# A two-layer transformer stack: inputs sent in pieces between the first weight units, modulation tiles and weight conversions placed between the rows of the first norm

## The reference, cut to what matters

```
m = silu(cond) @ ada_w[layer] + ada_b[layer]        # 3072 values, once for x and once for ctx
shift, scale, gate = split(m, 3)
h = rms_norm(x, norm_g) * (1 + scale) + shift       # 1024 wide; the same for ctx with its own values
x = x + gate * mixer(h)
```

## Time and profile before

| what | us |
|---|---|
| runs | 2254.93, 2245.04, 2248.68 (median 2248.68) |
| the profiled execution: its own time | 2256.99 |
| its span, first to last instruction | 2254.8 |
| busy: TensorE | 1992.5 (88%) |
| busy: VectorE | 1171.8 (52%) |
| busy: ScalarE | 887.4 (39%) |
| busy: GpSimd | 694.8 (31%) |
| mean granted TensorE clock | 0.926 |

### The profile page before, as it was taken

The page is one execution under the profiler, slowest core; times in us unless marked ns, Lnnn a source line. Parts: engine busy times, 40 slices in busy tenths (PEclk is TensorE's granted clock), DMA queues, the critical chain, the costliest instruction groups (busy, mean ns, idle before and its releaser), DMA issues.

```text
span 2254.8 us, 27585 instructions
## 1 busy us (share of the span) xinstructions
PE 1992.5 (88%) x10708; PEld 1606.3 (71%) x10708; DVE 1171.8 (52%) x1657; ACT 887.4 (39%) x1199; POOL 694.8 (31%) x310
## 2 busy tenths in 40 slices
PE   4899999999787977976683999999999999999996
PEld 3687677777666867764472788788778877878875
DVE  2422666664276757657799334225444464522442
ACT  3252656654334453443331444234432234422432
POOL 1121011102214223222235344344344443444432
PEclk6799999999978989878796999999999999999998
DMA  7111211212211100112120222223223322323331
GB/s 277 38 56 54 76 48 67 76 67 85 59 37 37 39 29 29 38 52 80 37 76 10 84 84 94 88 96 98 84 87 101 93 89 90 94 84 94 94 94 47
DMA packets 46257, 166.80 MB, mean 74 GB/s; under 512 B 5392, under 2 KB 5520, under 8 KB 45872
## 3 DMA queue, kind: packets, MB, share of 16 engines
q1 hardware_dynamic: 44208, 158.88, 22.1%
q10 hardware_dynamic: 1920, 6.16, 0.8%
HBM read 162.92 MB, written 2.10 MB: 73 GB/s over the span
## 4 chain that ended last, share of the span: by engine, by line
PE 75%; DVE 17%; ACT 4%; issue 2%; DMA 1%; POOL 0%; ACTq 0%; DVEq 0%
PE ps L454 20%; PE ps L455 20%; PE ps L456 20%; PE ps L559 4%; PE ps L572 2%; PE ps L589 2%; DVE ex L1210 2%; DVE sq L1210 2%; DVE hf L1210 2%; ACT sq L831 1%; DVE tmp L1210 1%; PE ps L488 1%; DVE acc L1210 1%; PE ps L476 1%; DVE wS L1605 1%
## 5 line engine op out<-in xcount | busy, mean ns | idle before, releaser
L1194 POOL TENSOR_TENSOR wlo<-raw,whi 128x1024 fp32r<-128x1024 f32 x251 | 607.7, 2434 | 1303.8 <-ACT whi L814 1303.8
L814 ACT ACTIVATE whi<-raw 128x1024 fp32r<-128x1024 f32 x251 | 257.7, 1055 | 669.1 <-PE ps L456 647.2
L454 PE MATMUL ps<-Ahi,whi 128*128 128x512 f32 (+1 forms) x784 | 320.1, 408 | 27.5 <-issue 11.9
L455 PE MATMUL ps<-Alo,whi 128*128 128x512 f32 (+1 forms) x784 | 314.9, 402 | 0.0
L456 PE MATMUL ps<-Ahi,wlo 128*128 128x512 f32 (+1 forms) x784 | 313.5, 400 | 0.0
L1210 DVE TENSOR_TENSOR ps<-ps,rstd 128x1024 f32<-128x1024 f32 (+1 forms) x60 | 69.7, 1162 | 263.8 <-PE ps L456 227.3
L454 PEld LDWEIGHTS ps<-Ahi,whi 128*128 128x128 f32 x784 | 154.8, 197 | 72.5 <-issue 23.0
L454 PE MATMUL ps<-Fhi,whi 128*128 128x512 f32 x416 | 167.5, 403 | 13.1 <-DVE Flo L1210 12.9
L456 PEld LDWEIGHTS ps<-Ahi,wlo 128*128 128x128 f32 x784 | 154.6, 197 | 33.7
L455 PEld LDWEIGHTS ps<-Alo,whi 128*128 128x128 f32 x784 | 154.9, 198 | 32.1 <-issue 0.5
L1216 DVE SCALAR_TENSOR_TENSOR cv<-ps,vec,cv 128x511 f32<-128x511 f32 (+1 forms) x176 | 131.9, 749 | 71.6 <-ACT cv L831 66.9
(11 more groups left out here) (252 smaller groups left out, 3919.9 us busy)
## 6 DMA issues: line engine op xcount, KB each, us to landing
raw<-in_units SPq DMA_DIRECT2D x299, 512.0 KB, 3.7
X<-in_xT ACTq DMA_DIRECT2D x1, 2048.0 KB, 12.8
out_xT<-X SPq DMA_DIRECT2D x8, 256.0 KB, 2.1
CX<-in_ctxT ACTq DMA_DIRECT2D x1, 1024.0 KB, 15.7
masks<-in_masks ACTq DMA_DIRECT2D x1, 512.0 KB, 3.5
acc<-in_rope ACTq DMA_DIRECT2D x1, 384.0 KB, 3.0
gmw<-in_gmw ACTq DMA_DIRECT2D x1, 384.0 KB, 2.9
bs<-in_bs ACTq DMA_DIRECT2D x1, 384.0 KB, 3.5
```

The lines of the kernel that those rows point to most:

```text
L454: nc.tensor.matmul(out, sh, mh, start=first, stop=False)
L455: nc.tensor.matmul(out, sh, ml, start=False, stop=False)
L814: nc.scalar.activation(whi[:, s % CONV, :], raw[:, c % RAW, :], ACT.Copy).then_inc(sem("whi"), 1)
L1194: nc.gpsimd.tensor_tensor(wlo[:, s % CONV, :], raw[:, plan.unit_at[("split", s)] % RAW, :], whi[:, s % CONV, :].bitcast(fp32), ALU.subtrac ...
```

## The change

1. **Input and constants.** X and CX are no longer sent by ScalarE's queue. SP sends them in four pieces of two rows each (256 KB a row of X, 128 KB a row of CX), piece i ahead of unit i+1. ScalarE's queue sends vec, sel, eps1, ident; `vec` has a semaphore of its own, and the first LOG_EXP table load goes.
2. **Order of the modulation tiles.** `ADA` orders them by row: shift 0, scale 0, shift 1, scale 1 and so on, then the gates of layer 0 and all of layer 1. `sc1` is made per scale tile, in `ada_t`. The norm's sum n0 comes after tile 1 and not after tile 7.
3. **VectorE's prologue.** One square sum, tiles 0 and 1, the other sums; then for each further tile its copy, the bias of the tile before, and one row.
4. **A row** is two instructions for hf = (X·sc1)·rstd, ScalarE adds the shift while it rounds (`shifted`, two instructions in place of one), and the remainder is (hf + shift) - high in two instructions in place of one.
5. **First weights.** Units 0, 1 and 2 of the converted weights are converted by ScalarE after rows 4, 5 and 6 (at most one each), and lowered by GpSimd then; before, all three came ahead of the norm's root.
6. **Attention and second norm.** Twelve modulation tiles stay in attention (both of pairs 0, 4, 5 and 6, that of q = 4 in pairs 1, 2 and 3, that of q = 0 in pair 7). The last four, tiles 8 to 11 of layer 1 (its gates), move behind l0: three ahead of the sum n1, one behind it, then their `ada_t`. Their units now stand between l0's and r's in the load order.

```
+ADA = [(0, 0), (0, 4), (0, 1), (0, 5), (0, 2), (0, 6), (0, 3), (0, 7)]
+ADA += [(0, j) for j in range(8, 12)] + [(1, j) for j in range(12)]
+ADA_BESIDE = {(p, q): i + 8 for i, (p, q) in enumerate([(0, 0), (0, 4), (1, 4), (2, 4), (3, 4), (4, 0), (4, 4), (5, 0),
+                                                        (5, 4), (6, 0), (6, 4), (7, 0)])}
+SS_AFTER = 1
+INPUTS_AT = {1: 0, 2: 1, 3: 2, 4: 3}
...
         for m in range(8):
             tile(("l0", m), [("residc", m + 1)], ktiles("wout0", m))
+        for i in range(20, 23):
+            ada(i)
         norm("n1")
+        ada(23)
+        for i in range(20, 24):
+            ada_t(i)
...
             for c, (kind, i) in enumerate(plan.units):
+                if c in INPUTS_AT:
+                    two = slice(2 * INPUTS_AT[c], 2 * INPUTS_AT[c] + 2)
+                    sy.dma_start(X[:, two, :], a["xT"][:, two, :]).then_inc(sem(f"in{INPUTS_AT[c]}"), 16)
+                    sy.dma_start(CX[:, two, :], a["ctxT"][:, two, :]).then_inc(sem(f"in{INPUTS_AT[c]}"), 16)
...
-            for j in range(8):
-                ada(0, j)
-                if j == 0:
-                    pe.wait_ge(sem("consts"), 16 * 4)
+            for i in range(8):
+                ada(i)
+                if i == 0:
+                    pe.wait_ge(sem("consts"), 16 * 3)
+                    pe.wait_ge(sem("ones"), 2)
                 else:
-                    ada_t(0, j - 1)
-            ada_t(0, 7)
-            pe.wait_ge(sem("ones"), 2)
-            norm("n0")
+                    ada_t(i - 1)
+                if i == SS_AFTER:
+                    norm("n0")
+            ada_t(7)
...
-                    if q in (0, 4):
-                        ada(*more[2 * p + q // 4])
-                    if q in (2, 5):
-                        ada_t(*more[2 * p + q // 4])
+                    if (p, q) in ADA_BESIDE:
+                        ada(ADA_BESIDE[p, q])
+                    if (p, q // 4 * 4) in ADA_BESIDE and q in (2, 5):
+                        ada_t(ADA_BESIDE[p, q // 4 * 4])
...
-            ac.dma_start(X[:, :, :], a["xT"]).then_inc(sem("xl"), 16)
-            ac.dma_start(CX[:, :, :], a["ctxT"]).then_inc(sem("cl"), 16)
-            nc.scalar.preload_act_table_set(LOG_EXP)
...
+            def shifted(layer, dst):
+
+                ac.wait_ge(sem("hf"), split[0] + 1)
+                k, b = dst
+                for c, cols in enumerate([slice(0, T), slice(T, N)]):
+                    act(b[:, k, cols], hf[:, split[0] % 2, cols], ACT.Identity, mod[:, layer, 2 * k + c:2 * k + c + 1], 1.0,
+                        "hi" if c else None)
+                split[0] += 1
+
+            squares("n0", both, lambda k: [(f"in{k // 2}", 32)])
+            ac.wait_ge(sem("consts"), 48)
+            root("n0", False)
             for k in range(KD):
-                high(Hhi[:, k, :])
+                shifted(0, (k, Hhi))
+                if k in (4, 5, 6):
+                    convert(plan.index[("adaT", 7)], 1)
...
+                if shift is None:
+                    tt(lo, hf[:, i % 2, 0:lo.shape[-1]], hi.bitcast(fp32), SUB, "lo")
+                else:
+                    for c, cols in enumerate([slice(0, T), slice(T, N)]):
+                        stt(lo[:, cols], hf[:, i % 2, cols], shift[:, c:c + 1], hi[:, cols].bitcast(fp32), ADD, SUB,
+                            "lo" if c else None)
...
+            def modulated(layer, k, hi, lo):
+                b = to_split(N)
+                for c, (src, cols) in enumerate([(X, slice(0, T)), (CX, slice(T, N))]):
+                    stt(b[:, cols], src[:, k, :], sc1[:, layer, 2 * k + c:2 * k + c + 1], rstd[:, cols], MUL, MUL,
+                        "hf" if c else None)
+                queued(hi[:, k, :], lo[:, k, :], mod[:, layer, 2 * k:2 * k + 2])
...
+            def ada_t(i):
+                layer, j = ADA[i]
+                ps = psum(("adaT", i))
                 tt(mod[:, layer, 4 * j:4 * j + 4], ps[:, 0:4], v_(f"ada_b{layer}", 4 * j, 4), ADD, "mod")
+                if 4 <= j < 8:
+                    c = slice(4 * j - 16, 4 * j - 12)
+                    stt(sc1[:, layer, c], mod[:, layer, 4 * j:4 * j + 4], 1.0, v_(f"norm_g{layer}", 4 * j - 16, 4), ADD, MUL)
...
-            ve.wait_ge(sem("consts"), 64)
-            sums("n0")
-            for j in range(8):
-                ada(0, j)
-                if j:
-                    ada_t(0, j - 1)
-            ada_t(0, 7)
-            scales(0)
-            modulated("n0", 0, Hhi, Hlo)
+            ve.wait_ge(sem("vec"), 16)
+            ada(0)
+            sums("n0", [1])
+            ada(1)
+            ada_t(0)
+            sums("n0", range(2, 8))
+            for i in range(2, 9):
+                if i < 8:
+                    ada(i)
+                ada_t(i - 1)
+                if i == 2:
+                    ve.wait_ge(sem("n_rs"), 2)
+                modulated(0, i - 2, Hhi, Hlo)
+            modulated(0, 7, Hhi, Hlo)
+            flush()
...
             sums("n1")
-            modulated("n1", 1, Ahi, Alo)
+            for i in range(20, 24):
+                ada(i)
+            ve.wait_ge(sem("n_rs"), 2 * NI["n1"] + 2)
+            for k in range(KD):
+                modulated(1, k, Ahi, Alo)
+                if k >= 4:
+                    ada_t(16 + k)
+            flush()
```

More of the change, by code:

```diff
@@ L127, in ada, with ada_t @@
                 self.ada += 1
-            tile(("ada", layer, j), [("arow", 12 * layer + j + 1)], slots=slots)
-        def ada_t(layer, j, slots=None):
-            tile(("adaT", layer, j), [("mod", 12 * layer + j + 1)], slots=slots)
+            tile(("ada", i), [("arow", i + 1)], slots=slots)
+        def ada_t(i, slots=None):
+            tile(("adaT", i), [("mod", i + 1)], slots=slots)
         def ktiles(name, m, k=KD):
@@ L173, in out @@
             tile(("O", p, q), [("og", TN * p + q + 1)], slots=[2])
-        more = [(0, j) for j in range(8, 12)] + [(1, j) for j in range(12)]
         score(0)
@@ L490, in ada @@
                 done(last)
-            def ada_t(layer, j):
-                ps = tile(("adaT", layer, j))
-                pe.wait_ge(sem("arow"), 12 * layer + j + 1)
+            def ada_t(i):
+                ps = tile(("adaT", i))
+                pe.wait_ge(sem("arow"), i + 1)
                 for m in range(2):
-                    last = nc.tensor.matmul(ps[:, 2 * m:2 * m + 2], arow[:, (2 * (j % 2) + m) * P:(2 * (j % 2) + m + 1) * P], sel[:, :],
+                    last = nc.tensor.matmul(ps[:, 2 * m:2 * m + 2], arow(i)[:, m * P:(m + 1) * P], sel[:, :],
                                             start=True, stop=True)
@@ L502, in _ @@
             pe.wait_ge(sem("cnd"), 1)
-            for j in range(8):
-                ada(0, j)
-                if j == 0:
-                    pe.wait_ge(sem("consts"), 16 * 4)
-                else:
-                    ada_t(0, j - 1)
-            ada_t(0, 7)
-            pe.wait_ge(sem("ones"), 2)
-            norm("n0")
+            for i in range(8):
+                ada(i)
+                if i == 0:
+                    pe.wait_ge(sem("consts"), 16 * 3)
+                    pe.wait_ge(sem("ones"), 2)
+                else:
+                    ada_t(i - 1)
+                if i == SS_AFTER:
+                    norm("n0")
+            ada_t(7)
             for m in range(5):
@@ L1223, in _, with sums @@
             nsq = [0]
-            def sums(name):
+            def sums(name, ks=None):
                 i = NI[name]
@@ L1231, in sums @@
                     ve.wait_ge(sem("psum"), plan.index[("ss", NORMS[i - 1][0])] + 1)
-                for k in range(1, k_):
+                for k in ks or range(1, k_):
                     ve.wait_ge(sem("n_sq"), nsq[0] + per * (k + 1))
@@ L1380, in _ @@
                         k_odd(p + 1)
-                    if q in (0, 4):
-                        ada(*more[2 * p + q // 4])
-                    if q in (2, 5):
-                        ada_t(*more[2 * p + q // 4])
+                    if (p, q) in ADA_BESIDE:
+                        ada(ADA_BESIDE[p, q])
+                    if (p, q // 4 * 4) in ADA_BESIDE and q in (2, 5):
+                        ada_t(ADA_BESIDE[p, q // 4 * 4])
             out(PAIRS - 1, TN - 1)
-            scales(1)
             def resid(key, m, gate=None, n_sem="resid"):
@@ L1400, in _ @@
             sums("n1")
-            modulated("n1", 1, Ahi, Alo)
+            for i in range(20, 24):
+                ada(i)
+            ve.wait_ge(sem("n_rs"), 2 * NI["n1"] + 2)
[4 more added lines that the diff above has]
+            flush()
+            ts(small2[:, 0:1], eps1[:, 0:1], 1.0, None, MUL, s="n_use")
             def decay(h, d):
```

96 lines of the change are left out of this document (42 added, 54 removed).

## The result

Measured with the kernel before on one chip, in turn: 2226.47 us (median of 4 runs, 2220.24 to 2230.62) against 2246.96, ratio 0.9894 with a 95% interval of 0.9866 to 0.9921, 20.5 us faster. The three have a mean of 25.7; 28.5 was predicted (2220.2 from the median shown). The profiled execution took 2220.24 us, with a span of 2218.5.

A forecast was written before the change was run, and what follows sets the result against it. TensorE was taken to bound mid-attention (busy 97.6 of 100 us), chains of waits the start and second norm. Gains of 18.5 + 6.5 + 3.5 = 28.5 us gave 2228.5 for the profiled execution, 2220.2 from the median; range 2210 to 2236.

The forecast's parts named there:

- Arrival and the norm: Start: tile 1's second unit lands near 15.2 us, square sums end near 24 (29.2 before), row 0 follows at 30.
- Rows between tiles: Prologue: VectorE sets the pace from 35.7 us, 2.6 us per row, rounds of 3.3; last remainder at 56.7 without collisions.
- Collisions: Rows 5 to 7: GpSimd's three lowerings and VectorE shut each other out, 7.0 us taken (bounds 0 and 7.0; 4.6 as seen).
- the first rival: Rows 5 to 7: lowerings beside VectorE cost nothing, 7.0 us more gained, gain 35.5, 2213 us; chance 0.16.
- c0: First product tile after the rows: ends between 64.7 and 66.4 us, 65.4 taken, against 83.9 before.
- First term: Start through the end of c0: 18.5 us gained, bounds 13 and 26.
- Attention: Four tiles taken out: three pairs give 2.1 us each, 6.3 together, and pair 7 gives 0.2.
- second term: Attention with four modulation tiles taken out: 6.5 us gained, bounds 0 and 10.
- The second rival: Attention gives nothing back, since ScalarE and VectorE pace its pairs and tiles filled holes: gain 22, 2226.7 us; chance 0.12.
- Second norm: Behind l0: shorter rows give 4.1 us, the fourth tile takes 0.5; 3.5 us gained, bounds 1 and 5.
- The rival on the other side: Slower: ScalarE's conversions in attention and at the second norm wait 4.7 us each for loads, 37.6 in all, 2257.8; chance 0.04.
- the third rival: Start: input pieces arrive out of order, sums 3.8 us late, late units 6.4 more; gain 18.3, 2230.4 us; chance 0.08.

The follow-up runs named there:

- The three: Changed kernel, unaltered, against the kernel before in three sets of runs on different chips: 20.5, 34.2 and 22.4 us faster.
- the second: Changed kernel, unaltered, against the kernel before once more on another chip: 2220.66 us (5 runs) against 2254.83 (11 runs), ratio 0.9853.

## Why the prediction was right

- **Arrival and the norm.** Tile 1's last unit landed at 17.0, not 15.2. The estimate took the bytes ahead of it over 0.40 MB/us; the third slice of 2.75 us has a dip to 201 that the kernel before doesn't have the earlier trace rows, some 0.5 MB or 1.4 us. It stands at 191 to 219 in all eleven profiles with the pieces in this order, at 285 with the pieces one unit earlier, and in neither of the two of the kernel before; why is open. GB/s in 40 slices of the changed kernel's first 110 us:

```profile
GB/s 53 375 201 398 419 419 416 413 307 0 6 179 374 334 389 393 356 273 0 191 21 173 34 162 0 0 191 0 0 191 0 6 186 4 0 182 9 0 0 6
```

The sums took 5.93 us as forecast and ended at 25.3, 1.3 late; row 0 began 1.6 late.
- **Rows between tiles.** 56.7 was forecast for the last remainder without collisions. Measured are 64.1 less 6.0, 58.1: 1.4 late, which the late arrival accounts for (row 0 was 1.6 late). Each three-operand instruction took 0.752 and 0.485 us, as the earlier trace rows had it, and three rounds of 3.3 us were seen as 3.27, 3.47 and 3.27. A unit's landing held a tile by only 0.17 us (at 43.50).
- **Collisions.** 7.0 was taken, 4.6 and 0 were the other values. It was 6.0, 2.0 per lowering (5.9 by the kernel without conversions between the rows, counted from row 5's start): the VectorE instruction that a lowering meets runs on to its end, up to 0.2 us, and the next one is held and ends 0.3 to 0.6 us after the lowering. VectorE had no idle time in which any of it could hide. By the rule of the Trainium skill ("SBUF — State Buffer", section "SBUF: two separate sides"), a VectorE instruction with two inputs in on-chip memory and a GpSimd one that reads it shut each other out, and the one that starts first holds the shared ports for its whole duration. The trace agrees, with 2.44 and 2.60 us in place of 0.485 beside lowerings of 2.42 and 2.38. That the collisions cost nothing, the first rival, is thereby out.
- **c0.** Forecast 65.4, measured 66.3, 65.1 and 66.8. That it comes so near is in part luck: the late arrival (1.4 to 1.6) and the smaller collisions (1.0) nearly cancel. First term 18.2 against 18.5. Of it the old rows would lack 3.8, by one run; the remaining 14.4 are the order.
- **Attention.** The step that failed is "second term: 6.5"; 4.2 was measured. For pairs 1 to 3 its mechanism was right, and 2.4 us per pair was rather more than the 2.1 taken. Pair 7 was wrong in sign: its tile was to give 0.2, and taking it out cost 0.6, since it had filled holes and the conversions moved. What was missing altogether is the clock: 1.6 us in pair 7, where TensorE's matmuls took 2.6 to 2.8 in place of 1.53 us behind a pause that was as long before, and the same again in pair 4 in one of three profiles, on top of 0.4 for a longer pause there. For the first profile that is 7.3 - 0.6 - 1.6 - 0.4 = 4.7, as measured (303.6 less 298.9). Where the clock held, with the old rows, attention gave 6.6, so the 6.5 of the sum is met there by two errors that cancel. The second rival, that attention gives nothing back, is out with 37.0 us against 39.4 per pair.
- **Second norm.** 3.5 was forecast, 4.0 measured: 4.9 for the rows (4.1 was worked out) less 1.0 for the tiles (0.5 worked out, and 0.5 for the unit that comes late, seen as a wait of 1.00). r's products began late, at 609.73, for TensorE had to wait for the first gate tile's bias; r's last steps caught up.
- **The rival on the other side.** No conversion in attention had an idle time ahead of it: all nine of ScalarE's weight conversions from 216 to 516 us (the prediction counted seven) follow their predecessors without one. Pieces arrived in order: squares went on at 9.16, 12.63 and 15.82 as each landed. That answers the third rival. Its 6.4 us for late units rested on a wrong reading: the 4.9 us in the earlier trace rows is how long the transfer ran, beside TensorE's work. The kernel before waited 0.26 us for it:

```profile
46.03 1.08 PE L488 MATMUL ps<-raw,cnd 128*32 128x128 f32 x16 [0.26 <-DMA raw<-in_units]
```

- **The number.** 18.2 + 4.2 + 4.0 and the differences in unchanged code (0.2 up to attention, -0.9 in l0) make 25.7, where the sum was 28.5. The changed kernel's median of 2226.47 lies within the range of 2210 to 2236, 6.3 above the 2220.2 forecast, and that number alone would fit the second rival's 2226.7 as well; only the pairs' times tell the two apart. That the first comparison gave 20.5 and the second 34.2 fits the scatter of the stretch behind the second norm, but it isn't shown: only one execution of each set has a profile, and the medians of the kernel before, 2246.96, 2254.83 and 2248.96, differ by 8 us on three chips.

## What to carry to other kernels

Where GpSimd and VectorE both read fp32 tensors from on-chip memory, count a GpSimd instruction as if it ran on VectorE (here 2.0 of 2.4 us each), and put only those beside VectorE's critical work whose result is used at once: the first unit was worth its collision, the other two weren't. Before sums or copies are interleaved with tiles, ask which of them the critical chain needs first; the square sums had been put behind a tile's transfer that they didn't need, which cost 3 us. And compare kernels by stages that end at a common instruction, since a long unchanged stretch behind the change can scatter by more than the change is worth.

## What the runs showed of the hardware that was not expected

- **The clock behind a pause.** With the same code and the same pause of 1.64 us, 24 matmuls took 1.53 us in three profiles and 2.57 to 2.83 in eleven; the three have the old rows in common, and no code of attention. Why the clock falls in the others is open.
- **The recorded clock and the durations.** Between 30 and 42 us the changed kernel's windows give a granted clock of 1.00, while a tile takes 1.93 us and its `ada_t` 1.01, exactly as before, where that stretch has a granted clock of 0.50. In the second profile of the kernel before the record says 1.00 there too, with the same 1.93 and 1.01. With the sums first a tile takes 1.08 at 27.7 us and its `ada_t` 0.61, and 1.93 and 1.01 again at 36.9, where the record has 0.50. The durations were taken for the clock here, and the record wasn't.
- **One tensor operand isn't safe either.** In the kernel with the old rows the scale-and-shift of a row, which reads a single tensor, is stretched from 0.55 to 2.44 and 2.54 us beside a lowering:

```profile
50.61 2.44 DVE L1249 TENSOR_SCALAR hf<-hf,sc,mod 128x512 f32<-128x512 f32 x1
...
61.33 0.55 DVE L1249 TENSOR_SCALAR hf<-hf,sc,mod 128x512 f32<-128x512 f32 x1
```

- **l0 takes 65.7 or 67.4 us** and nothing between; the kernel before has both, so the two values come with no edit. The cause is open.
